# Latent attention on one core: the later pairs' queries, keys and values split by ScalarE and VectorE straight from PSUM

## What is computed

```python
def mla_queries(c_q, q_norm_g, w_uq, rope):
    q = (rms_norm(c_q, q_norm_g) @ w_uq).reshape(B, L, MLA_HEADS, MLA_QK)
    q_nope, q_rope = q[..., :MLA_NOPE], q[..., MLA_NOPE:]
    if rope is not None:
        q_rope = apply_axial_rope(q_rope, *rope)
    return jnp.concatenate([q_nope, q_rope], axis=-1) * MLA_QK ** -0.5

# keys: 64 rows of c_kv @ w_ukv and 32 rotated rows shared by all heads; values: 64 columns
s = jnp.einsum('bqhd,bkhd->bhqk', qi, k)
p = jax.nn.softmax(s, axis=-1)
o = jnp.einsum('bhqk,bkhd->bqhd', p, v)
```

## Time and profile before

| | |
|---|---|
| median of 3 runs | 3948.91 us (3945.37 to 3950.83) |
| profiled execution, its time | 3948.27 us |
| profiled execution, its span | 3946.4 us |
| busy, share of the span: PE, DVE, ACT, POOL | 92%, 54%, 36%, 35% |
| attention steps, layer 0 | from 653 us, about 400 us |
| attention steps, layer 1 | from 2624 us, about 340 us |

### The profile page before, as it was taken

How to read it: one execution, slowest core, us unless ns; L and a number is a source line. 1 busy time by engine, 2 the same in 40 slices (tenths; PEclk the granted TensorE clock), 3 DMA queues, 4 the chain that set the end, 5 groups by cost and what they waited for, 6 DMA issues and landing times. The chain is left out here.

```text
span 3946.4 us, 53247 instructions
## 1 busy us (share of the span) xinstructions
PE 3643.4 (92%) x19584; PEld 3058.6 (78%) x19584; DVE 2129.9 (54%) x3793; ACT 1417.4 (36%) x2845; POOL 1366.5 (35%) x1239
## 2 busy tenths in 40 slices
PE   7989997999779899999999899969996989999997
PEld 3668996777667688888888679958886768888886
DVE  5468435666676444444444583356676555544544
ACT  3341125666513522222222412246672252222222
POOL 1121122555100055454554421126630005544554
PEclk8989977999889999999999899879998999999999
DMA  5245201001324111111111162010014311111111
GB/s 206 104 168 186 82 4 41 12 8 40 122 78 163 43 43 32 32 43 43 43 32 32 69 202 79 4 39 10 6 39 165 150 43 50 52 48 43 53 52 49
DMA packets 153895, 266.96 MB, mean 68 GB/s; under 512 B 8968, under 2 KB 122777, under 8 KB 151290
## 3 DMA queue, kind: packets, MB, share of 16 engines
q1 hardware_dynamic: 143452, 212.38, 16.2%
q0 software_dynamic: 6352, 46.01, 3.0%
q10 hardware_dynamic: 3920, 6.29, 0.5%
HBM read 229.10 MB, written 33.59 MB: 67 GB/s over the span
## 5 line engine op out<-in xcount | busy, mean ns | idle before, releaser
L2990 POOL TENSOR_TENSOR x<-x,mlp_tmp 128x512 f32<-128x512 f32 x576 | 785.3, 1394 | 1323.7 <-DVE mlp_tmp L2971 1318.5
L2971 DVE TENSOR_TENSOR mlp_tmp<-psum,gate 128x512 f32<-128x512 f32 x576 | 391.7, 689 | 273.1 <-POOL x L2990 194.5
L152 PE MATMUL psum<-act_hi,w_hi 128*128 128x512 f32 (+1 forms) x1280 | 472.6, 369 | 14.4 <-DVE w_lo L2949 14.4
L153 PE MATMUL psum<-act_lo,w_hi 128*128 128x512 f32 (+1 forms) x1280 | 472.3, 369 | 0.0
L154 PE MATMUL psum<-act_hi,w_lo 128*128 128x512 f32 (+1 forms) x1280 | 472.1, 369 | 0.0
L152 PE MATMUL psum<-w_hi,hidden_hi 128*128 128x512 f32 x1152 | 449.9, 391 | 0.0
L153 PE MATMUL psum<-w_lo,hidden_hi 128*128 128x512 f32 x1152 | 448.5, 389 | 0.0
L154 PE MATMUL psum<-w_hi,hidden_lo 128*128 128x512 f32 x1152 | 448.3, 389 | 0.0
L2963 DVE TENSOR_TENSOR hidden_lo<-square,hidden_hi 128x512 fp32r<-128x512 f32 x160 | 102.3, 639 | 591.9 <-ACT hidden_hi L2935 591.9
L1923 DVE TENSOR_REDUCE att_max<-psum 128x1 f32<-128x512 f32 (+2 forms) x272 | 217.4, 799 | 259.7 <-PE psum L154 259.5
L2927 ACT ACTIVATE relu<-psum 128x512 f32<-128x512 f32 x160 | 88.8, 555 | 666.0 <-PE psum L154 666.0
(11 more groups left out here) (386 smaller groups left out, 8238.6 us busy)
## 6 DMA issues: line engine op xcount, KB each, us to landing
w_raw<-in_mlp_w SPq DMA_DIRECT2D x128, 512.0 KB, 3.8
side_w<-in_w_ada SPq DMA_DIRECT2D x40, 1024.0 KB, 6.5
w_raw<-in_w_in SPq DMA_DIRECT2D x32, 512.0 KB, 4.8
hy_ahead<-in_hy_ahead POOLq DMA_DIRECT2D x8, 2048.0 KB, 12.6
open_tab<-in_hy_ahead POOLq DMA_DIRECT2D x8, 1024.0 KB, 13.0
spec_scratch<-open_staged SPq DMA_DIRECT2D x16, 512.0 KB, 2.7
hy_spec<-spec_scratch SPq DMA_DIRECT2D x16, 512.0 KB, 3.5
hy_back<-in_hy_back POOLq DMA_DIRECT2D x2, 4096.0 KB, 29.9
```

What stands on the lines that cost most here:

```text
L152: pe.matmul(out, lhs[0], rhs[0], start=start, stop=False)
L153: pe.matmul(out, lhs[0], rhs[1], start=False, stop=False)
L2971: dve.tensor_tensor(tmp[:, j % 2, :], ps[:, 4 + j % 4, :], gate[:, int(t >= LAT_TILES), 512 * h:512 * h + 512], ALU.mult).then_inc(gated.s ...
L2990: pool.tensor_tensor(a, a, tmp[:, j % 2, :], ALU.add).then_inc(added.sem, 1)
```

## The change

The later makes are now treated as the first ones: `high` on ACT and `low` on DVE read the bank itself, and queries of chunks 0 and 1 are rotated by DVE in the bank. `copy`, `split`, the buffers `make_raw`, `make_turned`, `make_hi` and the semaphores `copied` and `lo_p` are gone. PE's `bank_free` now waits for `low` of the past make (`lo_d`). In a step DVE does `rotate` first, ahead of `maximum(j, 0)`, and `low` after `probs_lo`, ahead of `invert`. ACT's `high` stands where `copy` stood; it is one instruction as before for q and v, and two for k, and for rotated queries it waits for `roped`. The waits for free slots of k, q and v go from POOL to ACT. `rope_part` and `k_rope` change places in SBUF. POOL keeps `norm`, `weights` and the loads for the next stage, which now wait for the last make itself.

```diff
             def high(m):
@@
                 elif kind == "q":
+                    h = p * PAIR + s
                     if c < 2:
                         act.wait_ge(roped.sem, roped[m])
-                    act.activation(qh[:, 0, cols], bank[0:MLA_QK, 0:n], ACT.Copy).then_inc(m_hi.sem, 1)
+                    if h >= Q_SLOTS:
+                        act.wait_ge(scored.sem, head_scored((h - Q_SLOTS) // PAIR, (h - Q_SLOTS) % PAIR))
+                    act.activation(qh[:, h % Q_SLOTS, cols], bank[0:MLA_QK, 0:n], ACT.Copy).then_inc(m_hi.sem, 1)
...
-            def copy(m):
-                act.wait_ge(made.sem, made[m])
-                if i >= RAWS:
-                    act.wait_ge(lo_p.sem, lo_p[later_makes[i - RAWS]])
-                act.activation(raws[i % RAWS][:, 0:n], bank_of(m)[:, 0:n], ACT.Copy).then_inc(copied.sem, 1)
...
                 if j - 1 in made_in:
-                    copy(made_in[j - 1])
+                    high(made_in[j - 1])
...
-                if j - 1 in made_in:
-                    split(made_in[j - 1])
-                    own(lo_p, lo_p[made_in[j - 1]])
...
                 if j - 1 in made_in and made_in[j - 1] == later_makes[-1]:
+                    pool.wait_ge(made.sem, made[later_makes[-1]])
                     hyena_first_loads(kit, l, pool)
...
+                if made_in.get(j - 1) in roped.at:
+                    rotate(made_in[j - 1])
                 if j < n_units:
                     maximum(j, 0)
...
                     if k not in early:
                         probs_lo(j - 2, k)
+                if j - 1 in made_in:
+                    low(made_in[j - 1])
                 if 0 <= j - 3 and j % 2 == 1 and j - 2 < n_units:
                     invert((j - 3) // 2)
...
                 if past in lo_d.at:
                     pe.wait_ge(lo_d.sem, lo_d[past])
-                elif past in copied.at:
-                    pe.wait_ge(copied.sem, copied[past])
```

More of the change, by code:

```diff
@@ L1659, in phase_latent @@
     made, m_hi, roped, lo_d = kit.sig("lat_made"), kit.sig("lat_hi"), kit.sig("lat_roped"), kit.sig("lat_lo")
[L1660 removed]
     made.plan(first_makes + later_makes)
[L1662 to L1666, removed]
+    m_hi.plan(first_makes + later_makes)
+    roped.plan([m for m in first_makes + later_makes if m[0] == "q" and m[3] < 2])
+    lo_d.plan(first_makes + later_makes)
     kr_spread = kit.sig("lat_kr_spread", 16, fresh=True)
@@ L1737, in high @@
                 else:
[L1738 to L1748 removed]
+                    if p >= 2:
+                        act.wait_ge(scored.sem, head_scored(p - 2, PAIR - 1))
+                    one = (p % 2) * PAIR
+                    act.activation(kh[0:MLA_NOPE, one, cols], bank[0:MLA_NOPE, 0:n], ACT.Copy)
+                    act.activation(kh[0:MLA_NOPE, one + 1, cols], bank[MLA_NOPE:P, 0:n], ACT.Copy).then_inc(m_hi.sem, 1)
             def exp(n):
@@ L1809, in weights @@
                 pool.tensor_tensor(uql[:], uq_raw[1][:], uqh[:].bitcast(F32), ALU.subtract).then_inc(w_lo.sem, 1)
[L1811 to L1827, removed]
-                    one, two = (p % 2) * PAIR, (p % 2) * PAIR + 1
-                    up, down = slice(0, MLA_NOPE), slice(MLA_NOPE, P)
-                    link(pool, pool.tensor_copy(kh[up, one, cols], raw[up, 0:n]))
-                    link(pool, pool.tensor_tensor(kl[up, one, cols], raw[up, 0:n], kh[up, one, cols].bitcast(F32), ALU.subtract))
-                    link(pool, pool.tensor_copy(other_hi[down, 0:n], raw[down, 0:n]))
-                    link(pool, pool.tensor_copy(kh[up, two, cols], other_hi[down, 0:n].bitcast(F32)))
-                    pool.tensor_tensor(kl[up, two, cols], raw[down, 0:n], other_hi[down, 0:n].bitcast(F32),
-                                       ALU.subtract).then_inc(lo_p.sem, 1)
-                else:
-                    h = p * PAIR + s
-                    slot = h % Q_SLOTS
-                    if c < 2:
-                        rows, other = slice(MLA_NOPE, MLA_QK), slice(MLA_QK, P)
-                        link(pool, pool.tensor_tensor(turned_rows[rows, :], raw[other, :], rot[other, cols], ALU.mult))
-                        link(pool, pool.tensor_tensor(raw[rows, :], raw[rows, :], rot[rows, cols], ALU.mult))
-                        link(pool, pool.tensor_tensor(raw[rows, :], raw[rows, :], turned_rows[rows, :], ALU.add))
-                    if h >= Q_SLOTS:
-                        pool.wait_ge(scored.sem, head_scored((h - Q_SLOTS) // PAIR, (h - Q_SLOTS) % PAIR))
-                    link(pool, pool.tensor_copy(qh[:, slot, cols], raw[0:MLA_QK, 0:n]))
-                    pool.tensor_tensor(ql[:, slot, cols], raw[0:MLA_QK, 0:n], qh[:, slot, cols].bitcast(F32),
-                                       ALU.subtract).then_inc(lo_p.sem, 1)
@@ L1907, in low @@
                     t0 = GROUPS[c][0]
-                    hi, lo = (v[0][:, t0:t0 + tiles_, :, a] for a in range(2))
+                    hi, lo = (v[p % 2][:, t0:t0 + tiles_, :, a] for a in range(2))
                     last = dve.tensor_tensor(lo, shaped(bank), hi.bitcast(F32), ALU.subtract)
```

28 lines of the change are left out of this document (16 added, 12 removed).

## The result

The changed kernel takes 4001.18 us (median; 3999.16 to 4004.01) against 3949.87 us for the kernel before, measured beside it: a ratio of 1.0131, with a 95% interval of 1.0116 to 1.0146. It is 51 us slower, where 43 were forecast, and lies within the range. The profiled execution's span grew from 3946.4 to 3998.4 us.

What follows compares the result with a forecast made beforehand. PE sets the attention stages' pace, held by DVE's chain to the transposes. Rotation 21.1 us plus late banks 22.0 us make 43.1 us on the profiled 3948.3: forecast 3991 us, 1.1% slower, range 3972 to 4008.

Steps and rivals of the forecast that it cites:

- The chain of step 15: Step's start, score, maximum, probs_lo, transposes: DVE holds PE until 2.34 us into the step, so a late maximum delays PE equally.
- rival A: DVE's idle time in the attention stages takes in all its new work, so the time stays at 3948; chance 0.09.
- The rotation, 21.1 us: 28 rotations on DVE delay the first maximum and so PE: 12.3 us in layer 0, 8.8 in layer 1.
- The ordinary term: In each ordinary step with a rotation the maximum, and with it PE, is 0.65 us late.
- the 1.32 for the pair of instructions: DVE's two rotation instructions take 1.32 us until the next starts, so rotation runs from 0.20 to 1.52 into the step.
- step 10: Layer 0, each pair: weigh waits for out, queued behind high, which waits for the rotation; PE is 1.46 us late.
- Step 2 of layer 0: Rotation costs 0.65 us, and the make, with nothing weighed yet, starts 1.65 us late for its bank.
- Step 1: With no probs_lo yet, half the rotation's delay is hidden: 0.36 us lost in both layers.
- rival C: Rotation's second instruction meets POOL's norm at the port each time: up to 20 us more, 4011; chance 0.05.
- The bank, 22.0 us: Makes wait for DVE's low of the past make to free the bank: 13.1 us in layer 0, 8.9 in layer 1.
- The signs: What the changed timeline would show, including PE's waits on DVE in both stages up some 40 us, on ACT hardly.
- rival B: Without split, DVE's two-SBUF-input instructions such as L1936 stop waiting for POOL's port: 16 us, time 3932; chance 0.04.

Runs made afterwards that it cites:

- the two told above: The changed kernel with ACT's out ahead of high, 4000.67 us; and the same with probability parts 0 and 1 ahead of rotation and first maximum, 3967.73 us.

## Why the prediction was right, and where it was not

*Only the attention stages change, and PE's wait for DVE is what grows:* right. 47.6 of 52.0 us are there. What is outside can't be laid to the change: from the last score of layer 0 to the first of layer 1, with the same code, the profiled executions took from 1580.7 to 1589.8 us in thirteen kernels, 1584.2 in the kernel before and 1589.7 in the changed one. Each kernel was traced once, so whether this scatter goes with the kernel or with the execution is not shown. The kernel before alone ran in anything from 3933.7 to 3954.1 us. Differences of about 5 us between two medians can therefore not be laid to an edit, and the steps, which repeat to 0.04 us where the clock is up, are the better witness.

*The chain of step 15:* right in every link. DVE's idle time did not help (rival A).

*The rotation, 21.1 us:* the stages give 21.5, which is near by luck: clock dips in both kernels stand in it, and the terms below it erred both ways. By the steps the 24 places of the later pairs cost 21.9 for 19.1. The ordinary term was 0.65 and measured 0.85 to 0.88. The step that failed is the 1.32 for the pair of instructions, which was read at the first rotation, whose successor starts 0.61 after the second instruction. In 27 of the 28 later ones the successor starts 0.73 after it (740.85 to 741.58 above), so that the pair takes 1.46, and the maximum's successor starts 0.70 after the maximum, not 0.61 (741.58 to 742.28; the earlier trace rows). Together 0.2 in each. The bound of 0.80 was too low as well. The longer spacing could have been read in the kernel before, at the next rotation of the same view:

```profile
646.75 0.70 DVE L1898 TENSOR_TENSOR psum<-rope_part 32x512 f32<-32x512 f32 x1
647.49 1.71 DVE L1916 TENSOR_TENSOR qT_lo<-psum,qT_hi 96x512 fp32r<-96x512 f32 x3
```

Here the successor starts 0.74 after the second instruction. Why the overlap with the next instruction is lost is open.

The other error is step 10, 0.99 for 1.46. The mechanism was as put: `weigh` starts 3.30 after the step's start for 1.88, 1.42 late. But PE had waited 0.13 for `exp` further on in that step, 1.42 less the 1.29 by which it grew, which the delay takes in, and step 11 is 0.30 shorter for a later start. The prediction said that no later wait would take a delay in; here two did. Step 2 of layer 0 is a third: its make started 5.58 after the step's start for 3.41, 2.17 late where 2.30 were forecast, but the step cost only 1.53, because in the kernel before the next score had waited as well:

```profile
663.09 0.50 PE L152 MATMUL psum<-kT_hi,qT_hi 96*128 96x512 f32 x1
...
667.95 0.50 PE L152 MATMUL psum<-kT_hi,qT_hi 96*128 96x512 f32 x1 [0.49 <-ACT probs L1757]
```

Step 1 was put at 0.36 in both layers and cost 0.18 and 0.01. In layer 1 the sum of steps 1 and 2 fits (1.08 for 1.01) by luck: step 2 holds the collision told under rival C.

*The bank, 22.0 us:* right place by place in the later pairs, with 0.98 measured as 1.08 to 1.10 for keys and all others within 0.1; together 20.9 for 20.3. Two kernels show it, one that adds only this and one that shortens it. Its share in step 2 of layer 0, put at 1.65, was not measured by itself at the full clock. Between the bank and the rotation nothing was hidden in the later pairs.

*The signs:* PE's waits for DVE should have grown by some 40 us and those for ACT hardly; they grew by 24 and by 9, of which most is step 9, booked to `exp`, and step 10, booked to `out`. The chain is the one forecast, and its last link has another name there.

*POOL's and ACT's relief is worth nothing:* right. L1936, now L1893, fell to its own duration everywhere, as rival B had it:

```profile
L1893 DVE TENSOR_TENSOR att_sums<-att_sums x64: 144/149/152, 675.2 to 3021.6; 128x2 f32<-128x2 f32 x64
```

Its longest was 873 ns. In step 11 of layer 1, where nothing else changed, it had taken 0.64 in each pair, and the step has the same length as before (6.70): the freed port bought no time.

*Rival C* did not occur as put: `norm` comes later than the rotation in the changed kernel. But POOL's splitting of the next weights met one rotation, in step 2 of layer 1:

```profile
2666.52 0.61 POOL L1801 CAST w_uq_hi<-uq_raw 128x512 fp32r<-128x512 f32 x1
...
2666.68 1.01 DVE L1853 TENSOR_TENSOR psum<-rope_part 32x512 f32<-32x512 f32 x1
```

Again DVE ends 0.56 after POOL. Three reorders made `norm` meet it too: the two told above, and the rotation in the middle with `out` first (1.11 for 0.70, in step 10 of layer 1). A meeting costs DVE 0.22 to 0.54 and not 0.73.

*What was missed in the prediction altogether* is that PE's wait in the kernel before was worth removing for itself: the rows that showed DVE as the last link also showed `probs_lo` queued behind an instruction that waits, with its own data long ready.

## What to carry to other kernels

Ask of an engine with idle time in which order it works within a step, not how busy it is: DVE, busy for 61% of the stage, was PE's last link in 37 places of it, 1.46 us of new work ahead of a maximum cost 0.87 us in an ordinary step, and putting the ready work ahead of the waiting one gained 12 us in the tuned kernel. Count who frees a PSUM bank and when: ACT's one copy, which freed it early, was worth about 22 us, and the work that it left to POOL cost nothing. When an instruction gets a new wait, look at what stands behind it in its queue (here ACT's `out`) and at what an earlier release sets free to collide with (here POOL's `norm`).

## What the runs showed of the hardware, unexpected

A wait of PE can be charged twice. Behind 2.60 us of idling the granted clock was 0.57 over 4 us, and 256-wide matmuls followed each other after 0.21 instead of 0.12 us. Not every wait does this: the changed kernel's three waits of 2.3 us in the steps 9 left the clock of these steps at 1.00, and over each of its stages it was 0.98 or more.

A step of the same code could differ by 1.6 to 1.8 us from one kernel's trace to another's by a dip of the clock, so that one step in one execution proves little. These dips are not all chance. The one in step 4 of layer 0 stands in the kernel before and in the kernel with only keys and values changed, whose first steps are the same, and in none of the eleven others, all of which changed step 2. A wait of 1.20 us for `exp` stands ahead of step 4 in the kernel before and in the changed one alike, and the clock behind it was 0.71 in the one and 1.00 in the other. What decides is open.

Two neighbouring instructions of DVE overlap by about 0.08 us in some places and not in others: behind the rotation's second instruction (0.70) the next one starts after 0.61 where it is a `kT_lo` of the first makes, and after 0.73 in front of a maximum. A term that is paid 28 times should be read at the neighbours that it will have.

An exclusive port between DVE and POOL charges what is left of the other's instruction. Wherever the rotation's second instruction, an add with two SBUF inputs, took longer than its 0.70, it ended 0.55 to 0.57 us after an instruction of POOL did, whether that was a multiply, a cast or a subtraction. It goes the other way too. In the kernel with the rotation in the middle and `out` first DVE's add was first in step 16, and POOL's multiply took 1.20 for 0.73 and ended 0.59 after it:

```profile
754.03 0.70 DVE L1853 TENSOR_TENSOR psum<-rope_part 32x512 f32<-32x512 f32 x1
754.12 1.20 POOL L1814 TENSOR_TENSOR att<-att_o_hi,att_rec 64x256 f32<-64x256 f32 x1
```
